# Output projections of the attention stages summed block by block between the attention's own work, in four banks, and idle products kept in the second half of the rows only

## The chip, the cores and the metric

One core of one Trainium2 chip runs the whole program. The time is device microseconds (us) for one execution. The time before is the median of three runs.

## What is computed

Two transformer blocks, one after the other, on 512 rows of 1024 features in float32. The first block (an attention, a recurrence, a convolution and a mixture that gathers 128 rows of two tables for each token) is not changed. The second block has two layers; each is a mixer, a cross attention on 256 memory rows, and a gated feed-forward part, and each of the three adds into the residual X:

```python
for layer in range(DEPTH_2):
    x = x + mixers[layer](rms_norm(x, mix_norms[layer]))     # ends in o @ w_out
    x = x + memory_cross_attention(rms_norm(x, xn), ...)      # ends in o @ w_o
    x = x + swiglu(rms_norm(x, fn), wg, wu, wd)
```

The even mixer (layer 0) has 8 heads of sliding-window attention and 8 heads of latent attention; the odd one (layer 1) has 16 heads of dilated attention; the cross attention has 4 heads of 128. The products that end the first two lines, `o @ w_out` and `o @ w_o`, are the "projections onto X" of this case.

## The kernel before

Each engine has its own program, written by the same generators, and they meet through semaphores (`p.wait_ge`, and `p.claim`, which waits for the last user of a bank or a weight slot). Every engine takes its instructions in the order written.

**Two halves.** The second block runs twice, on rows 0 to 255 (the first half, `h == 0`) and on rows 256 to 511 (the second half, `h == 1`). The first half is woven into the end of the first block's table gathers (`peer_steps`, `Beside`): POOL issues the gathers, DVE multiplies and adds the gathered rows (lines L2361 and L2375), and between them all engines take steps of `second_pe`, `second_act`, `second_dve` for half 0 in a fixed proportion of costs. In this execution that is about 1943 to 3145 us. The second half runs alone, from there to the end.

**Attention units.** An attention stage is a list of units (one head, 128 query rows): 32 in each mixer, 8 in each cross attention. For unit u the order on PE is: scores of u+1 (L2955), a piece of "fill", transposes of the weights of u (L2964), output of u-1 (L2973), and, where a block of 128 output columns is complete, its transpose into `a.o` (L2979, the store). DVE and ACT take the minimum, the exponent and the copies. The fill is PE work from a generator (`latent_pe`, `dilated_pe`: projections that later units need) of which `Fill.take` hands out `rate` steps a unit; a step `"after", n` is held until unit n. The steps are numbered the same way on ACT and DVE, which only yield there.

**Idle products.** Where a unit got little fill, `occupied` (L2658) issues a product of the identity by itself into bank 0, whose result nobody reads. It does so too, 8 at a time, before and after the row norm's products (`scale_pe`, L2733), and 2 before a rotation.

**Projection onto X.** `out_pe` runs after the last unit. It goes over four column groups i of 256, each with its own weight load of 1024 KB (512 KB in the cross attention), into banks 6 and 7 by turns; each group takes two chains over all blocks c of `a.o` (8, or 4 in the cross attention), by L2687. DVE adds group i into X (L2721) while PE is at group i+1, ACT squares it (L2706), DVE sums the squares (L2713), and `scale_pe` needs all of that.

**Weights** land in four wide slots taken in turn (`next_wide`); SP issues a load when the last user of the slot has ended (`load_wide`), in program order.

## Time and profile before

| | |
|---|---|
| median of 3 runs | 4248.45 us (4247.49 to 4258.28) |
| the profiled execution: its time, its span | 4260.14 us, 4258.3 us |
| PE busy | 3555.5 us (83%) |
| DVE, POOL, ACT busy | 2219.7, 1379.1, 711.5 us |
| mean granted clock of TensorE | 0.910 |
| second block, first half, beside the gathers | about 1943 to 3145 us |
| second block, second half, alone | about 3160 to 4258 us |

A granted clock of 1.0 in a row is TensorE at 2.4 GHz, 0.5 is 1.2 GHz, and a value between is a mean over a stretch that had both. A logical float32 product shows as two MATMUL records, so x8 in the order of a program is x16 in a timeline.

### The profile page before, as it was taken

The numbers are of one execution on the slowest core, as the hardware profiler recorded it, in microseconds if no ns is written. First come the engines' busy times: TensorE is split into PE (matmuls) and PEld (weight loads), VectorE is DVE, ScalarE is ACT, GpSimd is POOL, SyncE is SP. The second block draws the span as 40 slices with busy tenths as digits, with TensorE's granted clock in tenths as the row PEclk, the third lists the DMA queues.
The fourth block names the chain that finished last, engine by engine and source line by source line (L and its number), as shares of the span: only waits on it lengthen the run. The fifth ranks groups of instructions, "written<-read, shape, count | busy, mean of one in ns | idle before, by whom it ended". The sixth has DMA issues, their size and how long they took to land. (4 is left out here: it accounts for less than half of the span.)

```text
span 4258.3 us, 41827 instructions
## 1 busy us (share of the span) xinstructions
PE 3555.5 (83%) x15638; PEld 2641.1 (62%) x15638; DVE 2219.7 (52%) x4375; ACT 711.5 (17%) x1582; POOL 1379.1 (32%) x1215
## 2 busy tenths in 40 slices
PE   7888997888667677866788898888978899999999
PEld 3446557786323343425567776677766678877787
DVE  2443134445887878777667668777642420033201
ACT  2212122221211111111221001210011210012100
POOL 0550012221566666765235655445500000000000
PEclk9888988999888898979788999799988999999999
DMA  6320300004899899998567999779941134421343
GB/s 197 96 81 11 95 21 1 1 12 135 290 331 331 327 355 334 361 334 296 172 223 280 394 386 352 249 262 383 394 156 57 40 96 152 148 79 60 99 150 108
DMA packets 452351, 835.74 MB, mean 196 GB/s; under 512 B 46707, under 2 KB 294574, under 8 KB 452142
## 3 DMA queue, kind: packets, MB, share of 16 engines
q0 software_dynamic: 147456, 536.94, 34.3%
q1 hardware_dynamic: 304694, 296.13, 21.9%
q8 instruction: 125, 2.05, 0.2%
q14 instruction: 76, 0.62, 0.0%
HBM read 830.80 MB, written 2.17 MB: 196 GB/s over the span
## 5 line engine op out<-in xcount | busy, mean ns | idle before, releaser
L2687 PE MATMUL banks<-arena 128*128 128x256 f32 (+1 forms) x4992 | 1142.1, 388 | 78.3 <-DMA arena<-in_l_w_up 35.4
L2687 PEld LDWEIGHTS banks<-arena 128*128 128x128 f32 (+1 forms) x4992 | 954.9, 194 | 254.3 <-issue 40.9
L2246 POOL DMA_INDIRECT arena<-in_peer_u,arena x512 | 569.2, 1112 | 578.2 <-DVE arena L2375 226.3
L2246 POOL DMA_INDIRECT arena<-in_peer_v,arena x512 | 588.8, 1150 | 446.0 <-DVE arena L2361 284.9
L2375 DVE CUSTOM_DVE_ANT_0 arena<-arena 128x1024 f32<-128x1024 f32 x512 | 627.9, 1226 | 106.1 <-DMA arena<-in_peer_u,arena 89.1
L2319 PE MATMUL banks<-arena 128*128 128x512 f32 x768 | 419.6, 690 | 233.1 <-ACT arena L2337 150.0
L2319 PEld LDWEIGHTS banks<-arena 128*128 128x128 f32 x768 | 156.6, 217 | 461.0 <-issue 265.7
L2361 DVE SCALAR_TENSOR_TENSOR arena<-arena 128x1024 f32<-128x1024 f32 x316 | 406.2, 1286 | 34.9 <-DMA arena<-in_peer_v,arena 24.9
L3465 PE MATMUL banks<-arena 128*128 128x256 f32 x1408 | 310.4, 378 | 0.0
L3507 DVE TENSOR_TENSOR arena<-banks,arena 128x512 f32<-128x512 f32 x44 | 30.4, 692 | 526.7 <-PE banks L2687 526.3
L3465 PEld LDWEIGHTS banks<-arena 128*128 128x128 f32 x1408 | 265.6, 189 | 38.3
L2658 PE MATMUL banks<-arena 128*128 128x128 f32 x1088 | 189.0, 302 | 0.0
L2658 PEld LDWEIGHTS banks<-arena 128*128 128x128 f32 x1088 | 171.3, 217 | 22.2 <-issue 16.9
L835 PE MATMUL banks<-arena 128*128 128x512 f32 (+1 forms) x320 | 134.1, 567 | 28.4 <-ACT arena L962 11.7
L3486 ACT ACTIVATE arena<-banks 128x512 f32<-128x512 f32 x44 | 26.3, 599 | 698.5 <-PE banks L2687 698.4
L548 PE MATMUL banks<-arena 128*128 128x512 f32 (+1 forms) x384 | 142.1, 530 | 0.0
L3002 ACT ACTIVATE arena<-arena 128x256 f32<-128x256 f32 (+3 forms) x128 | 69.4, 542 | 374.1 <-DVE arena L3041 271.2
L2955 PE MATMUL banks<-arena 64*128 64x256 f32 (+6 forms) x384 | 124.8, 430 | 3.0 <-issue 2.3
L2063 PE MATMUL banks<-arena 128*128 128x512 f32 (+1 forms) x320 | 119.8, 526 | 3.5 <-ACT arena L1841 3.5
L835 PEld LDWEIGHTS banks<-arena 128*128 128x128 f32 x320 | 63.3, 207 | 92.9 <-issue 81.4
L1566 POOL TENSOR_TENSOR arena<-arena 64x256 f32<-64x256 f32 x24 | 19.1, 796 | 313.4 <-ACT arena L1465 312.5
L510 POOL TENSOR_TENSOR arena<-arena 128x2048 f32<-128x2048 f32 x16 | 57.3, 3603 | 194.0 <-ACTq L278 105.5
(330 smaller groups left out, 4326.4 us busy)
## 6 DMA issues: line engine op xcount, KB each, us to landing
arena<-in_l_w_gate SPq DMA_DIRECT2D x44, 1024.0 KB, 6.7
arena<-in_l_w_up SPq DMA_DIRECT2D x44, 1024.0 KB, 10.0
arena<-in_l_w_down SPq DMA_DIRECT2D x44, 1024.0 KB, 5.5
arena<-in_ada_w SPq DMA_DIRECT2D x24, 1024.0 KB, 8.1
arena<-in_l_w_qkv SPq DMA_DIRECT2D x24, 1024.0 KB, 8.2
arena<-in_w_in SPq DMA_DIRECT2D x36, 512.0 KB, 4.0
arena<-in_l_w_out SPq DMA_DIRECT2D x16, 1024.0 KB, 5.3
arena<-in_peer_q_w SPq DMA_DIRECT2D x20, 512.0 KB, 7.1
```

The source lines that it names most:

```text
L548: ins = p.e.matmul(k.bank[b][0:m, 0:n], k.W[slot][:, c, 0:m], rhs(c), start=c == 0, stop=c == c_n - 1, skip_group_check=True)
L835: ins = p.e.matmul(k.bank[b][0:m, 0:n], k.W[slot][:, c, 0:m], rhs(c), start=c == 0, stop=c == c_n - 1, skip_group_check=True)
L2063: ins = p.e.matmul(k.bank[4][:, cols], ws[j][:, c, :], k.HT[:, c, cols], start=c == 0, stop=c == DC - 1, skip_group_check=True)
L2246: p.e.indirect_dma_start(e.ring[slot], None, tables[table], bass.IndirectOffsetOnAxis(ap=e.IDX[h][:, t, j:j + 1], axis=0)).then_inc(*p.up( ...
L2319: ins = p.e.matmul(k.bank[b], e.diag[x % 4], e.ring[slot][:, half * T:half * T + T], start=h == 0 and j == 0, stop=h == HEADS - 1 and j == ...
L2361: p.e.scalar_tensor_tensor(out=e.ACC[t], in0=e.ring[slot], scalar=factor, in1=e.ACC[t], op0=ALU.mult, op1=ALU.add).then_inc(*p.up(S.rows_a ...
L2375: p.e.tensor_tensor_reduce(out=e.prod, in0=e.ring[slot], in1=e.H2[:, t, :], scale=1.0, scalar=0.0, op0=ALU.mult, op1=ALU.add, accum_out=e. ...
L2658: p.e.matmul(k.bank[0][:, 0:P], k.ident, k.ident, start=True, stop=True, skip_group_check=True)
L2687: ins = p.e.matmul(out, left(c), right(c), start=c == 0, stop=c == c_n - 1, skip_group_check=True)
L2955: ins = p.e.matmul(k.bank[b][:, c0:c0 + keys.shape[1]], x.q, keys, start=True, stop=True, skip_group_check=True)
L3002: p.e.activation(s[:, 0:x.nb], s[:, 0:x.nb], ACT.Exp, bias=low, scale=-1.0, accum_out=cols[:, 2:3]).then_inc(*(p.up(S.weights_exp, key) if ...
L3465: ins = p.e.matmul(k.bank[4 + o // 2][:, o % 2 * TH:o % 2 * TH + TH], w[:, r, P * o:P * o + P], a.hid[:, (i - 1) % 2, TH * r:TH * r + TH], ...
```

## The change

`out_pe` is cut in two. The blocks of `a.o` but the last are multiplied as soon as they are stored, as more fill among the units (`out_begun_pe`, `out_more_pe`); `out_pe` keeps the last block only. Since every block now adds into all four column groups, four banks (0, 1, 6, 7) stay open and all four weight slots are held from the first block to the last product.

```diff
+OUT_BANKS = 0, 1, 6, 7
+FIRST_PAIRS, LAST_PAIRS = (0, 1), (2, 3)
+WINDOWS_OUT, LATENTS_OUT = range(4), range(4, 7)
+def even_rate(u):
+    return 1 if u < 24 else 3
+def out_begun_pe(k, p, a, tag, stores, w, parts, cs):
+    for i in parts:
+        w[i] = landed_wide(k, p, (tag, i)).rearrange("p (c n) -> p c n", n=256)
+    for c in cs:
+        yield "after", stores[c][1] + 3
+        for stored in stores[c][0]:
+            p.wait_ge(*stored)
+        for i in parts:
+            bank = k.bank[OUT_BANKS[i]]
+            if c == 0:
+                p.claim(("bank", OUT_BANKS[i]), k.S.residual_added, (tag, i))
+            for x in range(2):
+                p.e.matmul(bank[:, TH * x:TH * x + TH], w[i][:, c, P * x:P * x + P], a.o[:, c, :], start=c == 0 and x == 0,
+                           stop=False, skip_group_check=True)
+            if i % 2:
+                yield 4 * MM
...
-def occupied(k, p, n):
+def occupied(k, p, a, n, b):
+    if a.h_id == 0:
+        return
+    if ("bank", b) in p.over:
+        p.wait_ge(*p.over["bank", b])
     for _ in range(n):
-        p.e.matmul(k.bank[0][:, 0:P], k.ident, k.ident, start=True, stop=True, skip_group_check=True)
+        p.e.matmul(k.bank[b][:, 0:P], k.ident, k.ident, start=True, stop=True, skip_group_check=True)
...
-    yield from units_pe(k, p, a, ("even", h), even_units(k, a), Fill(latent_pe(k, p, a)), 1)
-    yield from out_pe(k, p, a, ("mix", h), stores_of(k, ("even", h), even_units(k, a)))
+    begun = lambda parts, cs: out_begun_pe(k, p, a, ("mix", h), stores, w, parts, cs)
+    fill = chain(latent_pe(k, p, a, begun(FIRST_PAIRS, WINDOWS_OUT)), begun(LAST_PAIRS, WINDOWS_OUT),
+                 out_more_pe(k, p, a, stores, w, LATENTS_OUT))
+    yield from units_pe(k, p, a, ("even", h), units, Fill(fill), even_rate)
+    yield from out_pe(k, p, a, ("mix", h), stores, w, (DC - 1,))
...
-            yield from units_pe(k, p, a, ("dil", h), dilated_units(k, a), Fill(dilated_pe(k, p, a)), 2)
+            fill = chain(dilated_pe(k, p, a), out_begun_pe(k, p, a, ("l1_out", h), stores, w, range(4), range(DC - 1)))
+            yield from units_pe(k, p, a, ("dil", h), units, Fill(fill), dilated_rate)
...
-        yield from cross_pe(k, p, a, l)
-        yield from units_pe(k, p, a, ("cross", l, h), cross_units(k, a, l), none(), 0)
+        yield from cross_pe(k, p, a, l, 0)
+        fill = chain(cross_pe(k, p, a, l, 1), [("cross", l, h)], out_begun_pe(k, p, a, ("xo", l, h), stores, w, range(4), range(3)))
+        yield from units_pe(k, p, a, ("cross", l, h), units, Fill(fill), cross_rate)
```

ACT and DVE get the same steps without the products. In the cross attention the second half of the query projection (`cross_pe(..., 1)`) moves among the units too. The idle products are 544 in the second block before (282 in the first half, 262 in the second), and none and 208 after. The sum of the step costs that sets the proportion of gathers to second-block work is the same.

Lines of the changed kernel that stand in the rows below: L2808 and L2831 are the products moved among the units, L2845 those left in `out_pe`, L2692 is L2687, L2663 is L2658, L2738 is L2733, and L3021, L3030, L3039, L3045 are scores, weights, output and store.

**Place 1.** PE, dilated attention of the second half, where the query, key and value projections have run out. Before, a unit there has idle products only:

```order
L2955 MATMUL banks<-arena 128x256 [waits scores_low]
L2955 MATMUL banks<-arena 128x256
L2979 MATMUL banks<-arena 128x128 [waits act_weights,output_scaled]
L2658 MATMUL banks<-arena 128x128
L2964 MATMUL banks<-arena 128x128 [waits dve_stored,weights_exp]
L2964 MATMUL banks<-arena 128x128 x2
L2658 MATMUL banks<-arena 128x128
L2973 MATMUL banks<-arena 128x64 x3
```

After, the last step of the value projection is followed, one unit further on, by block 0 of the projection (the four rows of a unit between are left out):

```order
L3021 MATMUL banks<-arena 128x256 [waits scores_low]
L3021 MATMUL banks<-arena 128x128
L2692 MATMUL banks<-arena 128x256 x8
L3021 MATMUL banks<-arena 128x256 [waits scores_low]
L3021 MATMUL banks<-arena 128x256
L3045 MATMUL banks<-arena 128x128 [waits act_weights,output_scaled]
L2808 MATMUL banks<-arena 128x256 [waits landed_wide3,landed_wide0,landed_wide2,landed_wide1]
L2808 MATMUL banks<-arena 128x256 x3
L2808 MATMUL banks<-arena 128x256 [waits values_ready]
L2808 MATMUL banks<-arena 128x256
L2808 MATMUL banks<-arena 128x256 [waits rotated]
L2808 MATMUL banks<-arena 128x256
```

What was two idle products is now 8 products in four banks, and ahead of them PE waits for four weight slots.

**Place 2.** PE, cross attention of the second half, layer 1. Before, the whole query projection stands ahead of the units:

```order
L2687 MATMUL banks<-arena 128x256 [waits residual_added,landed_wide2]
L2687 MATMUL banks<-arena 128x256 x15
L2955 MATMUL banks<-arena 128x256 [waits cross_ready]
L2955 MATMUL banks<-arena 128x256 [waits norm_root]
L2658 MATMUL banks<-arena 128x128
L2964 MATMUL banks<-arena 128x128 [waits weights_exp]
L2964 MATMUL banks<-arena 128x128
```

After, its last four products stand among the units, and the next scores wait for `cross_ready` and for all four weight slots:

```order
L2692 MATMUL banks<-arena 128x256 x4
L3030 MATMUL banks<-arena 128x128 [waits act_stored,weights_exp]
L3030 MATMUL banks<-arena 128x128
L3039 MATMUL banks<-arena 128x128 x2
L2692 MATMUL banks<-arena 128x256 x4
L3021 MATMUL banks<-arena 128x256 [waits landed_wide2,landed_wide1,cross_ready,landed_wide0,landed_wide3]
L3045 MATMUL banks<-arena 128x128 [waits act_weights,output_scaled]
L2808 MATMUL banks<-arena 128x256 [waits dve_stored]
L2808 MATMUL banks<-arena 128x256 x3
```

The wait for the weights of the projection has moved from behind the units to unit 4.

**Place 3.** PE, end of the dilated stage of the second half. Before, the last store is followed by 64 products:

```order
L2979 MATMUL banks<-arena 128x128 [waits output_scaled]
L2687 MATMUL banks<-arena 128x256 [waits landed_wide1]
L2687 MATMUL banks<-arena 128x256 x6
L2687 MATMUL banks<-arena 128x256 [waits dve_stored]
L2687 MATMUL banks<-arena 128x256 x8
L2687 MATMUL banks<-arena 128x256 [waits landed_wide2]
L2687 MATMUL banks<-arena 128x256 x15
L2687 MATMUL banks<-arena 128x256 [waits residual_added,landed_wide3]
L2687 MATMUL banks<-arena 128x256 x15
L2687 MATMUL banks<-arena 128x256 [waits residual_added,landed_wide0]
L2687 MATMUL banks<-arena 128x256 x15
L2658 MATMUL banks<-arena 128x128 x8
```

After, it is followed by 8, which wait for the copy of that store:

```order
L3045 MATMUL banks<-arena 128x128 [waits output_scaled]
L2845 MATMUL banks<-arena 128x256 [waits dve_stored]
L2845 MATMUL banks<-arena 128x256 x7
L2663 MATMUL banks<-arena 128x128 [waits scores_low]
L2663 MATMUL banks<-arena 128x128 x7
L2738 MATMUL banks<-arena 128x256 [waits scores_low,residual_squared,residual_summed]
L2738 MATMUL banks<-arena 128x256 x3
```

The norm's four products (L2738) now stand 16 instructions behind the last store.

## Rows read from the trace of the kernel before

**Rows 1.** Windows by stage: busy us (instructions) by engine, granted clock, DMA share, GB/s
```profile
2031.00:2196.00 165.00, 118.01 (x483) 87.25 (x482) 102.03 (x267) 39.47 (x125) 37.34 (x39) 0.74 0.51 158
...
2250.00:2286.00 36.00, 24.48 (x106) 19.58 (x105) 20.38 (x45) 8.61 (x26) 8.90 (x10) 0.62 0.55 189
...
2723.00:2771.00 48.00, 39.22 (x147) 30.85 (x148) 28.99 (x81) 11.25 (x35) 14.93 (x13) 0.57 0.58 186
...
3245.00:3396.00 151.00, 120.65 (x578) 82.20 (x578) 61.62 (x209) 46.25 (x128) 0.00 (x0) 0.90 0.09 28
...
3881.00:3918.00 37.00, 30.78 (x211) 26.28 (x212) 15.77 (x54) 11.01 (x29) 0.00 (x0) 1.00 0.04 15
```

**Rows 2.** Timeline of PE, dilated attention of the second half: start, us, line, what, idle
```profile
3868.70 3.62 PE L2687 MATMUL banks<-arena 128*128 128x256 f32 x16
...
3874.38 3.72 PE L2687 MATMUL banks<-arena 128*128 128x256 f32 x16
...
3880.42 0.39 PE L2658 MATMUL banks<-arena 128*128 128x128 f32 x2
...
3881.55 0.52 PE L2964 MATMUL banks<-arena 128*128 128x128 f32 x3 [0.74 <-DVE arena L3074]
...
3917.74 27.89 PE L2687 MATMUL banks<-arena 128*128 128x256 f32 x128
...
3947.24 1.92 PE L2733 MATMUL banks<-arena 128*128 128x256 f32 x8
```

**Rows 3.** Timeline of PE, end of a feed-forward part of the second half
```profile
3717.15 1.95 PE L2658 MATMUL banks<-arena 128*128 128x128 f32 x16
...
3721.43 1.97 PE L2733 MATMUL banks<-arena 128*128 128x256 f32 x8 [2.33 <-ACT arena L2706]
```

**Rows 4.** Timeline of PE, even mixer of the second half
```profile
3324.95 0.39 PE L2658 MATMUL banks<-arena 128*128 128x128 f32 x2
...
3338.55 2.76 PE L3271 MATMUL banks<-arena 128*96 128x256 f32 x12
...
3374.83 0.39 PE L2658 MATMUL banks<-arena 128*128 128x128 f32 x2
...
3395.35 1.90 PE L2687 MATMUL banks<-arena 128*128 128x256 f32 x8
```

**Rows 5.** Timeline of PE, cross attention of the second half, layer 1
```profile
3966.61 1.03 PE L2955 MATMUL banks<-arena 128*128 128x256 f32 x4
...
3978.78 0.41 PE L2964 MATMUL banks<-arena 128*128 128x128 f32 x2 [0.87 <-ACT arena L3017]
...
3980.54 0.39 PE L2658 MATMUL banks<-arena 128*128 128x128 f32 x2
...
3989.87 14.02 PE L2687 MATMUL banks<-arena 128*128 128x256 f32 x64
...
4005.51 1.96 PE L2733 MATMUL banks<-arena 128*128 128x256 f32 x8
```

**Rows 6.** DMA issues of the second half alone: KB each, median us to landing
```profile
arena<-in_l_w_out SPq DMA_DIRECT2D x8, 1024.0 KB, 5.1
...
arena<-in_l_w_xo SPq DMA_DIRECT2D x8, 512.0 KB, 3.3
```

**Rows 7.** The same for the first half, beside the gathers
```profile
arena<-in_l_w_gate SPq DMA_DIRECT2D x22, 1024.0 KB, 19.4
...
arena<-in_l_w_out SPq DMA_DIRECT2D x8, 1024.0 KB, 9.4
```

**Rows 8.** Timeline of PE, first half: a wait and the speed after it
```profile
2955.46 8.77 PE L2687 MATMUL banks<-arena 128*128 128x256 f32 x32 [4.90 <-DMA arena<-in_l_w_up]
...
2964.07 6.21 PE L3465 MATMUL banks<-arena 128*128 128x256 f32 x28
...
1968.51 3.75 PE L2733 MATMUL banks<-arena 128*128 128x256 f32 x8 [9.84 <-DVE arena L2713]
```

**Rows 9.** Idle products of the first half: window of line L2658 alone
```profile
2031.00:2196.00 165.00, 33.24 (x138) 27.83 (x138) 0.74 0.51 158
```

More of the change, by code:

```diff
@@ new lines, in out_begun, with out_more_pe @@
+def out_begun(stores, parts, cs):
+    for c in cs:
+        yield "after", stores[c][1] + 3
+        for i in parts:
+            if i % 2:
+                yield 4 * MM
+def out_more_pe(k, p, a, stores, w, cs):
+    for c in cs:
+        yield "after", stores[c][1] + 3
+        for stored in stores[c][0]:
+            p.wait_ge(*stored)
+        for i in range(4):
+            for x in range(2):
+                p.e.matmul(k.bank[OUT_BANKS[i]][:, TH * x:TH * x + TH], w[i][:, c, P * x:P * x + P], a.o[:, c, :], start=False,
+                           stop=False, skip_group_check=True)
+            if i % 2:
+                yield 4 * MM
@@ L2788, in out_act, with out_pe @@
+def out_pe(k, p, a, tag, stores, w, cs):
+    for c in cs:
+        for stored in stores[c][0]:
+            p.wait_ge(*stored)
     for i in range(4):
         for x in range(2):
-            yield from product_pause(chunks)
+            for c in cs:
+                ins = p.e.matmul(k.bank[OUT_BANKS[i]][:, TH * x:TH * x + TH], w[i][:, c, P * x:P * x + P], a.o[:, c, :], start=False,
+                                 stop=c == cs[-1], skip_group_check=True)
+            if x:
+                ins.then_inc(*p.up(k.S.proj_filled, (tag, i)))
+            yield MM * len(cs)
@@ L2791, in out_act @@
+def out_act(k, p, a, tag, cs):
+    for i in range(4):
+        for x in range(2):
+            yield MM * len(cs)
             if i and x == 0:
@@ L2922, in stores_of @@
         if x.ends:
-            out.setdefault(x.block, []).append(((k.S.act_stored, k.S.dve_stored)[x.tile % 2], (name, u)))
+            out.setdefault(x.block, ([], u))[0].append(((k.S.act_stored, k.S.dve_stored)[x.tile % 2], (name, u)))
+            out[x.block] = out[x.block][0], u
     return out
@@ L2936, in units_pe @@
             filled = 0
-            for n in fill.take(rate, min(u + 1, len(units) - 1)):
+            for n in fill.take(rate(u), min(u + 1, len(units) - 1)):
                 filled += n
@@ L2988, in units_act @@
         if step == "fill":
-            yield from fill.take(rate, min(u + 1, len(units) - 1))
+            yield from fill.take(rate(u), min(u + 1, len(units) - 1))
         elif step == "rest":
@@ L3026, in units_dve @@
         if step == "fill":
-            yield from fill.take(rate, min(u + 1, len(units) - 1))
+            yield from fill.take(rate(u), min(u + 1, len(units) - 1))
         elif step == "rest":
@@ L3086, in rotate_pe @@
     n = out.shape[1]
-    occupied(k, p, 2)
+    occupied(k, p, a, 2, 1 if key[0] == "in" else 4)
     p.wait_ge(k.S.raw_ready, key)
@@ L3234, in latent_sp, with latent_pe @@
               ("latent_k", h, 3, 1))
-def latent_pe(k, p, a):
+def latent_pe(k, p, a, between):
     S, h = k.S, a.h_id
@@ L3288, in latent_pe, with latent_act @@
         yield "latent", h, i
-def latent_act(k, p, a):
+        if i == 1:
+            yield from between
+def latent_act(k, p, a, between):
     S, h = k.S, a.h_id
@@ L3324, in latent_act, with latent_dve @@
         yield "latent", h, i
+        if i == 1:
+            yield from between
 def latent_last(a, i):
     return ("even", a.h_id), 16 + 4 * i + 3
-def latent_dve(k, p, a):
+def latent_dve(k, p, a, between):
     S, h = k.S, a.h_id
@@ L3362, in latent_dve @@
         yield "latent", h, i
+        if i == 1:
+            yield from between
 def even_units(k, a):
@@ L3425, in cross_units @@
                  None, None, [(k.S.cross_ready, ("cross", l, a.h_id, i // 2))], (k.S.mem_ready, (l, 7)), True,
[L3426 removed]
+                 a.o[:, i, P * t:P * t + P], i, ("cross", l, a.h_id) if i >= 2 else None) for i in range(4) for t in range(2)]
 def ffn_sp(k, p, a, l):
@@ L3667, in second_pe @@
     p.turn = 0
-    none = lambda: Fill(iter(()))
     yield from experts_pe(k, p, a, ("experts", h))
@@ L3703, in second_act @@
     yield from inputs_act(k, p, a)
-    yield from units_act(k, p, a, ("even", h), even_units(k, a), Fill(latent_act(k, p, a)), 1)
-    yield from out_act(k, p, a, ("mix", h))
+    units = even_units(k, a)
+    stores = stores_of(k, ("even", h), units)
+    fill = chain(latent_act(k, p, a, out_begun(stores, FIRST_PAIRS, WINDOWS_OUT)), out_begun(stores, LAST_PAIRS, WINDOWS_OUT),
+                 out_begun(stores, range(4), LATENTS_OUT))
+    yield from units_act(k, p, a, ("even", h), units, Fill(fill), even_rate)
+    yield from out_act(k, p, a, ("mix", h), (DC - 1,))
     for l in range(2):
@@ L3731, in second_dve @@
     yield from inputs_dve(k, p, a)
-    yield from units_dve(k, p, a, ("even", h), even_units(k, a), Fill(latent_dve(k, p, a)), 1)
-    yield from out_dve(k, p, a, ("mix", h))
+    units = even_units(k, a)
+    stores = stores_of(k, ("even", h), units)
+    fill = chain(latent_dve(k, p, a, out_begun(stores, FIRST_PAIRS, WINDOWS_OUT)), out_begun(stores, LAST_PAIRS, WINDOWS_OUT),
+                 out_begun(stores, range(4), LATENTS_OUT))
+    yield from units_dve(k, p, a, ("even", h), units, Fill(fill), even_rate)
+    yield from out_dve(k, p, a, ("mix", h), (DC - 1,))
     for l in range(2):
```

111 lines of the change are left out of this document (58 added, 53 removed).

## The prediction

> **What bounds the kernel now.** The table of the profile comes first: PE is busy 83% of the span, the others 52% and less. Then the windows by stage, because an average says little here. In the second half of the second block (from about 3160 us) nothing but PE, its clock and the waits inside the attention matter: in the dilated units without fill PE is busy 30.8 of 37 us, some of it with idle products, DVE 15.8 and ACT 11.0, and the DMA share is 0.04 [rows 1]. In the first half the same units stand between gathered rows on DVE and take longer: 48 us instead of 37, at a granted clock of 0.57 instead of 1.00, and the even mixer 165 us instead of 151, at 0.74 instead of 0.90 [rows 1]. PE's clock is down there while PE is working, and the gathers leave DMA time over (share 0.51 to 0.58). The timeline of PE then shows what the change can win: the piece of a unit that no work covers. It is small, since a unit has only about 1.2 us of it.
>
> **Prices used everywhere.** 64 products of the projection take 27.89 us, so one is 0.434 us and one block c (8 products) 3.5 us [rows 2]. The stage from the last store to the norm's products is 3947.24 - 3917.74 = 29.5 us in a mixer [rows 2] and 4005.51 - 3989.87 = 15.6 us in a cross attention [rows 5].
>
> After the change that stage has 8 products. Its adds can't hide behind products any more: DVE adds, ACT squares, DVE sums, by turns. The end of a feed-forward part has this chain already, with four banks ending 0.87 us apart: 3721.43 - 3717.15 = 4.3 us from the last product to the norm's [rows 3]. Before, it was 1.8 us of idle products. The first of the 8 also waits for the last store's copy, which 8 products of older blocks covered before; a wait for that copy was 0.74 us [rows 2]. So the stage is 3.5 + 4.3 + 0.7 = 8.5 us. **A mixer** moves 56 products, 24.3 us: 24.3 + 8.5 - 29.5 = +3.3 us before anything is covered. **A cross attention** moves 24, 10.4 us: 10.4 + 8.5 - 15.6 = +3.3 us. That is a debt of 3.3 us in each of eight places, and units have to pay it back.
>
> Products that go over four banks by turns cost nothing extra: the down projection does that and runs 28 records in 6.21 us, 0.22 us each like the others [rows 8].
>
> **Second half, part by part.**
>
> Dilated: a unit with 8 products took 3874.38 - 3868.70 = 5.7 us, so its own work is 2.2; eleven without took 3917.74 - 3880.42 = 37.3, or 3.4 each [rows 2]. The 1.2 us between them are waits and idle products. Seven units get a block: -8.3. The fourth weight slot is that of the last value projection, so its load starts when that has ended and lands 5.1 us later [rows 6], one unit (2.2) of which is covered: +2.9, with all units queued behind that wait. 3.3 - 8.3 + 2.9 = **-2.1**.
>
> Even: the fill has room at two places. Four windowed units get 4 products (1.7 us) each; five took 3338.55 - 3324.95 = 13.6, 2.7 each [rows 4]; with own work of about 1.5 (rows of the cross attention, below) they become 3.2, so 6.9 us of products cost 2.0: -4.9. Of the last six units (3395.35 - 3374.83 = 20.5, 3.4 each, own work 2.2 as in the dilated ones) three get products: -3.6. The last weight slot is that of the key up-projection, which ends directly ahead of the wait: +5.1 [rows 6], and a wait of that length was followed by 8.77 us where 32 records take 7.0: +1.8 [rows 8]. 3.3 - 4.9 - 3.6 + 5.1 + 1.8 = **+1.7**.
>
> Cross: 8 units took 3989.87 - 3966.61 = 23.3 [rows 5]; a unit's own work is 3980.54 - 3978.78 = 1.8 less one idle product of 0.2, say 1.5 [rows 5]. Of 11 us free, the last unit's 1.2 stay: -9.8, filled with the 7 us of query products and 10.4 of the projection. Against it +3.3, +0.8 for the first scores, which now follow the ACT copy of their own queries at once (as a store's copy, 0.74), and +3.3 for the load of 512 KB into the slot of the second query part [rows 6]. **-2.4, twice: -4.8.**
>
> Sum of the second half: -2.1 + 1.7 - 4.8 = -5.2 us.
>
> **First half.** The same, and four differences.
>
> Longer units. They are 11 us longer in the dilated stage [rows 1], 7 of 11 are filled: -7. In the even mixer 14 us, 7 of 32: -3. In the first cross attention 36 us instead of 23 [rows 1]; DVE has gathered rows among these units, so of 13 us I take half, twice: -13.
>
> Slower loads. A projection's load lands after 9.4 us beside the gathers, not 5.1 [rows 7]: +4.3 in each mixer; in the cross attentions, where the DMA share is 0.55, I take 3 of the 6 us more: +6. Together +15. Also the four slots now come free within 3.5 us and not over 30, and the first feed-forward load (19.4 us to landing [rows 7]) is wanted 3.5 + 4.3 + about 6 us of norm later: some 5 us late; that stage fetches at the limit anyway, so +3 in all.
>
> No idle products. In the even mixer they are 69 (138 records), 33 us busy [rows 9]; records overlap, so some 16 us of PE, half of it in waits that stay: -8, and with the rest of the first half -10.
>
> The clock. Around a norm PE now rests for the whole chain. After a rest of 9.84 us the norm's 8 records took 3.75 us where they take 1.92 [rows 2, 8]: +1.8, and about +1 for the first products behind it (of the 1.8 of rows 8, part was there before). Six norms: +17, of which 5 are inside feed-forward stages that wait for weights: +12.
>
> Sum: -5.2 - 23 + 15 + 3 - 10 + 12 = -8 us.
>
> TensorE: Matmul & The Clock Gate (Part 1, The HAM clock gate) in the Trainium skill says that the low clock is the default and that activity releases it. By that rule taking idle products out of a stage whose clock is already 0.74 speaks against this change; my sum has it at the norms only, and with it in the units too the sum would be the second rival's. The trace agrees as far as rows 8 go.
>
> **Total:** -5.2 - 8 = -13 us on a profiled execution of 4260.1 us (span 4258.3), that is 4247. The median of the runs is 4248.45, 11.7 below that execution, so I put the difference on the median: **4236 us**. One execution more or less differs by about 0.3%, 12.7 us, and less than that is no change.
>
> **Rivals.**
>
> Clock low in the first half (slower). The units' own small products alone don't bring the clock back. PE was busy 118 us in the even mixer's window, 85 without the idle products' 33, at 0.74 [rows 1, 9]; at 0.5 it is 85 x 0.74 / 0.5 = 126, +41 us, less what lies in waits. 4236 + 41 = 4277 at most; at a mean of 0.62 it is +16, 4252. It decides from +25 us on, a clock under 0.57 there. For it: 0.57 in the dilated window although idle products ran. Against: units with real fill have more work, not less. Chance 0.21.
>
> Clock high in the first half. The moved products bring the clock to 1.0 where it is 0.57 to 0.74: the even window's 85 us become 63 (-22), the dilated window's own share of 39 becomes some 12 less; with the credits above, 4236 - 34 = 4202. For it: where fill of L2687 runs, the second half has 1.00. Chance 0.23.
>
> Loads eat the gain. The four waits last their full landing in both halves (5.1 and 9.4 us, none covered), and the feed-forward loads come 5 us late for each of gate and up: +3 in the second half, +12 in the first, 4251: no change. Chance 0.14.
>
> **How the numbers follow.** The forecast (4229 to 4244) has 0.42, half of it beyond 0.3%. Faster: 0.22 + 0.23 = 0.45. Same: 0.20, 0.12 of the loads' case and 0.02 of the low clock's, 0.34. Slower: 0.19 + 0.02 = 0.21. The low end of unknown costs is every credit in full and a clock of 1.0 (4198), the high end the low clock for most of the even mixer (4264); outside lie 2 in 10.
>
> **What would show it.** Right: from last store to the norm's products 8.5 us in the second half; a wait of PE for w_out of about 5 us late in the even mixer and 3 in the dilated stage, for w_xo 3 in each cross attention; units with 8 products at 5.7 us; norm products at 3.7 us in the first half. Wrong: a granted clock of the window of the first even mixer under 0.6 or over 0.9, or a chain of adds that is much longer where gathered rows stand between them on DVE.

## The result: 1.1% slower

The changed kernel took 4304.60 us (median of 4 runs, 4298.10 to 4309.00), the kernel before 4247.97 us (4 runs): a ratio of 1.0112, 95% interval 1.0084 to 1.0139. The prediction was 4236 us and a range to 4264, so it was wrong in sign and out of its range. The profiled execution took 4309.00 us, 48.9 more than that of before.

The head of the profile's page after the change (busy time, share, instructions, and the granted clock of PE in 40 slices):

```profile
span 4307.1 us, 40453 instructions
...
PE 3518.1 (82%) x14966; PEld 2580.3 (60%) x14966; DVE 2220.7 (52%) x4375; ACT 713.4 (17%) x1582; POOL 1363.6 (32%) x1215
...
PEclk9887988998888898888688998889988999999999
```

PE is busy 37 us less than before (no idle products in the first half), and the span is 49 us longer. So PE rests some 86 us more. The list of PE's waits (total, times, longest) names where:

```profile
PE banks L2738 <- ACT arena L2711: 48.6, 10, 13.4
...
PE banks L2738 <- issue: 21.0, 5, 7.3
PE banks L3021 <- DMA arena<-in_l_w_xo: 20.1, 4, 8.2
...
PE banks L2808 <- DMA arena<-in_l_w_out: 16.7, 3, 7.0
```

20.1 and 16.7 us are waits for the weights of the projections, which PE never waited for before. A fourth rest, 5.24 us before 3405.53, is put down to "issue" in the timeline. It is a wait for w_out too: the fourth load of w_out was issued at 3400.32 and landed at 3405.44. That makes 42.0 us in all. L2738 is the norm's products: their rests were 35.0 us before and are 69.6 here, which is most of the remainder.

Now the same stretches as in [rows 1] (the window ends are shifted, since everything comes later), and two pieces of the dilated tail by themselves:

```profile
core 0: us, PE busy (x) PEld busy (x) DVE busy (x) ACT busy (x) POOL busy (x), PEclk, DMA share, GB/s
2031.00:2219.00 188.00, 130.98 (x452) 90.01 (x450) 119.80 (x288) 39.73 (x125) 54.19 (x54) 0.70 0.57 180
2263.00:2300.00 37.00, 25.85 (x99) 19.61 (x100) 20.78 (x40) 3.65 (x13) 11.24 (x11) 0.77 0.55 171
2747.00:2810.00 63.00, 45.29 (x190) 35.68 (x190) 40.83 (x90) 8.15 (x29) 30.70 (x24) 0.80 0.65 213
3268.00:3447.00 179.00, 146.07 (x659) 103.38 (x658) 61.33 (x208) 46.70 (x128) 0.00 (x0) 0.89 0.07 24
3917.00:3983.00 66.00, 59.53 (x295) 49.90 (x295) 15.75 (x53) 11.47 (x29) 0.00 (x0) 0.87 0.02 7
3926.00:3954.00 28.00, 28.00 (x153) 23.84 (x151) 6.66 (x23) 5.44 (x14) 0.00 (x0) 1.00 0.00 1
3954.00:3968.00 14.00, 11.83 (x48) 9.62 (x47) 3.90 (x13) 2.63 (x8) 0.00 (x0) 0.62 0.00 0
```

The clock of the first even mixer is 0.70 and not far from the 0.74 of [rows 1]; in the cross attention and the dilated mixer of the first half it is higher than before (0.77 and 0.80, where it was 0.62 and 0.57). What the reader should see is the second half. There the dilated tail ran at 1.00 before; now it has 0.87, and behind 28 us in which PE is full come 14 us at 0.62.

The timeline of PE shows how a rest and a low clock go together. A row is start, duration, operation, and in brackets the rest before it:

```profile
3398.36 1.93 PE L3350 MATMUL banks<-arena 128*64 128x512 f32 x4 [0.95 <-DVE arena L3169]
3405.53 3.75 PE L2808 MATMUL banks<-arena 128*128 128x256 f32 x8 [5.24 <-issue]
...
3455.40 3.53 PE L2738 MATMUL banks<-arena 128*128 128x256 f32 x8 [2.29 <-issue]
...
3757.21 1.97 PE L2738 MATMUL banks<-arena 128*128 128x256 f32 x8 [2.33 <-ACT arena L2711]
...
3919.12 5.38 PE L2808 MATMUL banks<-arena 128*128 128x256 f32 x16 [2.74 <-DMA arena<-in_l_w_out]
...
3926.44 3.72 PE L2808 MATMUL banks<-arena 128*128 128x256 f32 x16
...
3932.15 3.62 PE L2808 MATMUL banks<-arena 128*128 128x256 f32 x16
...
3956.74 0.49 PE L2663 MATMUL banks<-arena 128*128 128x128 f32 x2 [1.44 <-ACT arena L3083]
...
3958.02 1.81 PE L3039 MATMUL banks<-arena 128*128 128x64 f32 x8
...
3967.93 5.24 PE L2808 MATMUL banks<-arena 128*128 128x256 f32 x16 [0.73 <-DVE arena L3140]
...
3982.39 0.33 PE L3045 MATMUL banks<-arena 128*128 128x128 f32 x1 [0.45 <-DVE arena L3134]
3983.10 3.72 PE L2845 MATMUL banks<-arena 128*128 128x256 f32 x16 [0.39 <-DVE arena L3140]
...
3990.90 3.16 PE L2738 MATMUL banks<-arena 128*128 128x256 f32 x8 [2.29 <-issue]
...
4020.22 1.19 PE L3021 MATMUL banks<-arena 128*128 128x256 f32 x2 [3.68 <-DMA arena<-in_l_w_xo]
...
4022.19 3.69 PE L2808 MATMUL banks<-arena 128*128 128x256 f32 x8 [0.57 <-DVE arena L3140]
...
4027.44 1.89 PE L2808 MATMUL banks<-arena 128*128 128x256 f32 x8
...
4031.22 1.99 PE L2808 MATMUL banks<-arena 128*128 128x256 f32 x8 [0.38 <-DVE arena L3140]
...
4034.77 1.89 PE L2808 MATMUL banks<-arena 128*128 128x256 f32 x8
```

8 records of L2808 take 1.89 us at full clock. Behind the waits of 5.24 and 3.68 us they take 3.7; behind the one of 2.74 us, 16 records take 5.38 us where they take 3.72 otherwise. The norm's products take 3.2 to 3.5 us behind an attention, where the same instructions took 1.92 before [rows 2].

**Where the time went, by stage.** A stage is taken from the start of one norm's 8 records to the next in the timeline (1970.28, 2229.81, 2309.26 and so on; before: 1968.51, 2227.86, 2301.44). Ahead of 1970.28 the change lost 1.8 us. From there to the first norm of the mixer in the second half (3211.53, before 3188.58) it lost 21.2, and from there to the last norm (4293.08, before 4243.80) 26.3, or 26.4 as the sum of the rounded stages:

| stage | first half | second half | predicted, second half |
|---|---|---|---|
| even mixer | +0.2 | +7.6 | +1.7 |
| cross attention, layer 0 | +5.9 | +3.7 | -2.4 |
| feed-forward, layer 0 | +1.8 | +1.5 | 0 |
| dilated mixer | +8.4 | +7.9 | -2.1 |
| cross attention, layer 1 | +4.6 | +4.1 | -2.4 |
| feed-forward, layer 1 | +0.2 | +1.6 | 0 |

(The two joints between the halves are +0.2 and 0.0.) Each kind of attention loses, in both halves. The second half, beside which no rows are gathered, is the cleaner one to explain.

### The profile page after: what moved, and what is told of

It is laid out like the page before. It is cut to its first block and busy times, and to the rows that moved or that the text cites. A ratio compares the mean times of both kernels' runs of the same rounds, so it can differ in the third digit from the quotient of the medians.

```text
span 4307.1 us, 40453 instructions
## 1 busy us (share of the span) xinstructions
PE 3518.1 (82%) x14966; PEld 2580.3 (60%) x14966; DVE 2220.7 (52%) x4375; ACT 713.4 (17%) x1582; POOL 1363.6 (32%) x1215
## 3 DMA queue, kind: packets, MB, share of 16 engines
q8 instruction: 120, 1.97, 0.2%
## 5 line engine op out<-in xcount | busy, mean ns | idle before, releaser
L2692 PE MATMUL banks<-arena 128*128 128x256 f32 x4224 | 982.7, 391 | 81.9 <-DMA arena<-in_l_w_up 36.5
L2692 PEld LDWEIGHTS banks<-arena 128*128 128x128 f32 x4224 | 817.1, 196 | 237.2 <-issue 53.9
L2246 POOL DMA_INDIRECT arena<-in_peer_v,arena x512 | 574.9, 1123 | 469.7 <-DVE arena L2361 311.4
L2319 PEld LDWEIGHTS banks<-arena 128*128 128x128 f32 x768 | 159.6, 221 | 460.1 <-issue 265.2
L3535 PE MATMUL banks<-arena 128*128 128x256 f32 x1408 | 310.4, 378 | 0.0
L3535 PEld LDWEIGHTS banks<-arena 128*128 128x128 f32 x1408 | 265.6, 189 | 38.3
L2808 PE MATMUL banks<-arena 128*128 128x256 f32 x544 | 153.5, 439 | 31.9 <-DMA arena<-in_l_w_out 16.7
L2808 PEld LDWEIGHTS banks<-arena 128*128 128x128 f32 x544 | 117.3, 223 | 58.7 <-issue 25.4
L3021 PE MATMUL banks<-arena 64*128 64x256 f32 (+6 forms) x384 | 124.4, 429 | 22.9 <-DMA arena<-in_l_w_xo 20.1
L3556 ACT ACTIVATE arena<-banks 128x512 f32<-128x512 f32 x44 | 26.3, 598 | 696.1 <-PE banks L2692 696.0
L3134 DVE TENSOR_SCALAR arena<-banks,arena 128x64 f32<-128x64 f32 (+1 forms) x160 | 47.6, 298 | 157.0 <-PE banks L3039 152.2
L3123 DVE COPY arena<-banks 128x128 f32<-128x128 f32 (+2 forms) x80 | 36.6, 457 | 173.8 <-PE banks L3030 173.8
```

The source lines that it names most:

```text
L2246: p.e.indirect_dma_start(e.ring[slot], None, tables[table], bass.IndirectOffsetOnAxis(ap=e.IDX[h][:, t, j:j + 1], axis=0)).then_inc(*p.up( ...
L2319: ins = p.e.matmul(k.bank[b], e.diag[x % 4], e.ring[slot][:, half * T:half * T + T], start=h == 0 and j == 0, stop=h == HEADS - 1 and j == ...
L2692: ins = p.e.matmul(out, left(c), right(c), start=c == 0, stop=c == c_n - 1, skip_group_check=True)
L2808: p.e.matmul(bank[:, TH * x:TH * x + TH], w[i][:, c, P * x:P * x + P], a.o[:, c, :], start=c == 0 and x == 0, stop=False, skip_group_check ...
L3021: ins = p.e.matmul(k.bank[b][:, c0:c0 + keys.shape[1]], x.q, keys, start=True, stop=True, skip_group_check=True)
L3535: ins = p.e.matmul(k.bank[4 + o // 2][:, o % 2 * TH:o % 2 * TH + TH], w[:, r, P * o:P * o + P], a.hid[:, (i - 1) % 2, TH * r:TH * r + TH], ...
```

## The experiments

Twelve kernels. Ratios are to the kernel before, timed on the same chip; the chips differ (the kernel before had medians of 4248, 4267, 4280 and 4257 us), so the ratios count, not the microseconds. Stage numbers are read as in the table above, and are of one profiled execution each. In the second half they repeat to 0.8 us where the code is the same, with three exceptions: the feed-forward part of layer 0 came out at 0.0 once and at +1.5 or +1.6 three times, and in the kernel before without idle products in its first half the cross attention of layer 0 took 2.6 us and the dilated mixer 23.7 us longer (told at the end). In the first half they repeat badly: the first half of the change gave +21 and +8 us in two profiles, and that of the kernel before came out 6.9 us shorter in a second one.

### Are idle products and the clock of the first half the cause?

Two kernels. The change with its idle products in both halves:

```diff
-    if a.h_id == 0:
-        return
```

> The changed kernel, with its idle products issued in both halves of the rows (the change issued none in the first half). Theory A, the waits for the weight loads of the projections make the loss (PE waits 26.8 us for them in the first half and 15.2 us in the second): the idle products move the time by less than 4 us, about 4304. Theory B, the missing idle products let the granted clock fall in the first half (0.70 in the even mixer where it was 0.74, norm products 3.3 to 3.6 us where they took 1.92): at least 10 us come back, 4294 or less, and the norm products there take 1.9 us again.

Ratio 1.0093 (1.0061 to 1.0126), which can't be told from 1.0112. The first half lost 21.7 us against 21.2. By the ratios anything from nothing to some 25 us may have come back, by the stages nothing did. Theory B falls with its other part too: the six norms behind a stage of the first half took 2.6 to 3.8 us, not 1.9, with idle products around them. These idle products come with the change's banks and waits, which the next but one experiment takes by themselves.

And the kernel before, without the idle products of its first half:

```diff
+    if a.h_id == 0:
+        return
```

> The kernel before, with only the idle products of the first half left out. Theory A (waits for loads): no difference over 0.3% from the kernel before, 4248. Theory B (clock): the clock falls without them, 10 us or more slower, 4258 or more. The prediction's own terms were -10 for the products and +12 for the norms, +2 together.

Ratio 0.9971 (0.9946 to 0.9996), if anything faster. The mean granted clock over all runs fell from 0.906 to 0.899, and the first half got 12.4 us shorter. The lower clock cost nothing that could be seen. The expectation had -10 and +12 here, +2 in all. The +12 had no occasion in this kernel: behind the attentions the whole projection still stands ahead of the norm, and the norm's products took 1.97 us as before. So -12.4 is to be set against the -10 alone, and agrees with it within the scatter of the first half. My slower rival (low clock in the first half) finds no support.

### The idle products' banks

The kernel before, with the change's banks and waits for the idle products:

```diff
+    if ("bank", b) in p.over:
+        p.wait_ge(*p.over["bank", b])
-        p.e.matmul(k.bank[0][:, 0:P], ...
+        p.e.matmul(k.bank[b][:, 0:P], ...
```

> The kernel before, with only the banks of the idle products as in the change (2, 4 and 5, 1 at the inputs) and the wait for the last user of that bank ahead of each. If an idle product can stand behind that wait as well as ahead of it: 4248, within 0.3%. Rival: the idle product that stood in the gap of a unit now stands behind it, the granted clock falls in the units that have no other fill as it did for 14 us in the changed kernel's second dilated stage (0.62), 8 us or more slower, 4256 or more.

Ratio 1.0049 (1.0020 to 1.0077), 21 us: the rival, not the main expectation. In the second half the even mixer lost 4.6 us, the dilated one 4.0, each cross attention 1.4. Two things make this up. In a unit the idle product stood in the rest, ahead of the wait; now it waits for a reader of its bank and stands behind it. In the dilated mixer, where [rows 2] has 0.39 us of idle products at 3880.42 and then 0.74 us of rest, the same place is now

```profile
3902.82 0.49 PE L2661 MATMUL banks<-arena 128*128 128x128 f32 x2 [0.88 <-DVE arena L3077]
3903.15 0.49 PE L2967 MATMUL banks<-arena 128*128 128x128 f32 x3
```

L2661 is the idle product. That costs 0.1 to 0.2 us a unit, 1.3 us over the eleven units there and 1.4 in a cross attention. The other part is the clock. At a rotation in the even mixer the kernel before has its idle products ahead of the rest, and this run has them behind it:

```profile
3361.16 0.61 PE L2658 MATMUL banks<-arena 128*128 128x128 f32 x4
3363.38 1.10 PE L3089 MATMUL banks<-arena 96*96 96x512 f32 x2 [1.62 <-ACT arena L3081]
...
3365.20 1.00 PE L2973 MATMUL banks<-arena 128*128 128x64 f32 x8
```

```profile
3374.67 0.71 PE L2661 MATMUL banks<-arena 128*128 128x128 f32 x4 [1.59 <-ACT arena L3020]
3375.21 1.14 PE L3092 MATMUL banks<-arena 96*96 96x512 f32 x2
...
3377.86 1.75 PE L2976 MATMUL banks<-arena 128*128 128x64 f32 x8
```

L3020 is ACT's copy out of bank 4. The rests are of one length, but the eight records behind them take 1.75 us and not 1.00; the window over these units has a clock of 0.84 (3371 to 3403), where it was 1.00 before (3358 to 3388). It isn't so at every such place: at a rotation of the dilated mixer (a rest of 1.53 us, 1.48 before) the 8 records of a projection behind it took 2.75 us, and 2.76 before. Of the dilated mixer's 4.0 us, 2.5 came ahead of the first idle product that waits for its bank: the norm's products and the first projections ran at the low clock there (2.81 us for the norm, 1.97 before), behind a rest of 2.33 us that both kernels have. That part is chance and not the banks, as the last section shows. So some 9 us of the 11.4 are a piece of the change that I had not priced.

With four banks held open there is no bank without another engine in it; the Trainium skill's PSUM — Partial Sum Buffer (Terms) says that two engines may not be in one bank of one quadrant at once, which no run here shows.

The other way round, the changed kernel with its idle products in bank 0 again, without a wait (while the sum stands open there, they multiply by a block of zeros):

```diff
+    left, begins = k.ident, True
+    if b in (4, 5):
+        b = 0
+        if getattr(p, "begun", False):
+            left, begins = k.K["causal"][:, 0:P], False
```

> The changed kernel, where the idle products of the units and rotations go to bank 0 without a wait again; while the projection's sum stands open there they multiply by zeros and add nothing. Theory D, an idle product behind the claim of bank 4 or 5 is on the path (the kernel before lost 4.6 us in the second even mixer, 4.0 in the dilated one and 1.4 in each cross attention by it): with some 100 such products left in the second half 4 to 6 us come back there, about 0.1% of the time, mostly in the two mixers. Rival: it was the clock by chance, nothing comes back in those stages.

The ratio, 1.0084 (1.0055 to 1.0114), can't tell it from the change, but the stages can: even mixer +3.1 us and not +7.6, the dilated one +7.3 and not +7.9, the cross attentions +3.8 and +3.7. The whole second half is +20.6 and not +26.4. The 5.8 us that came back were expected (4 to 6), but not "mostly in the two mixers": 4.5 are in the even one, where the change too has an idle product behind a rest of 1.59 us ahead of a rotation and a low clock after it. Where products fill the units there is little.

### The waits for weights

The changed kernel, with the identity in place of the weights in the products that were moved:

```diff
-                p.e.matmul(bank[:, TH * x:TH * x + TH], w[i][:, c, P * x:P * x + P], a.o[:, c, :], ...
+                p.e.matmul(bank[:, TH * x:TH * x + TH], k.ident, a.o[:, c, :], ...
```

> The changed kernel, where the products moved among the units take the identity matrix in place of the loaded weights, so that they wait for no load (only the last block's products still do, when the loads have long landed). The output is not the projection's; number, shape and place of all products are those of the change. Theory A (waits for loads): 42 us of waits go, and some 5 to 8 us of half clock behind them, 4254 to 4265, close to the kernel before. Rival C, the units have no room for the products and the waits only stand where PE would have waited for DVE anyway: less than 20 us come back, over 4285.

Ratio 0.9973 (0.9942 to 1.0003): against 1.0112, 1.4% or 59 us, where 47 to 50 were expected. The two intervals together leave some 17 us either way, but the stages say the same: PE's 42.0 us of waits were worth more than themselves, in the second half 23.8 us for 15.2. In the second half the even mixer went from +7.6 to -0.3 for a wait of 5.24 us, the cross attentions from +3.7 and +4.1 to -2.3 and -2.2 for 3.53 and 3.68 us. The dilated one stayed at +5.7, and the feed-forward part of layer 0 at +1.6.

Where does the wait have to stand? In `out_begun_pe` the four waits come when the generator is asked for its next step. In a cross attention that is ahead of the scores of unit 4, long before the first product is due. One edit moves them:

```diff
-    for i in parts:
-        w[i] = landed_wide(...)
     for c in cs:
         yield "after", stores[c][1] + 3
...
         for i in parts:
+            if i not in w:
+                w[i] = landed_wide(...)
```

> The changed kernel, where only one thing is moved: each column group's wait for its weight load stands ahead of its own first product, and no longer all of them ahead of the first unit's hold. Order and number of products are the change's. If the place of the wait is what costs in the cross attentions: their PE waits of 3.5 us in the second half and 8.2 and 4.8 in the first go nearly all, with half clock behind them 2 to 3 us each, some 25 us in all, 4280; the mixers, whose last group is wanted at once, keep most of theirs. If only the other order helps: under 8 us.

Ratio 1.0013 (0.9983 to 1.0043). I expected 25 us and got about 42 (the two intervals together leave some 17 either way): the place of one kind of wait is worth about as much as the whole loss. That doesn't make it the only cause: the second half is still +11.2 us, and the first half, which has no idle products now, came out at -9.3. In the second half the cross attentions are at -1.8 and -1.4, the feed-forward parts behind them at 0.0; PE waits for no w_xo at all. In the dilated mixer the wait went too, against the expectation. The even mixer keeps its wait and is +8.9:

```profile
3374.43 2.08 PE L2808 MATMUL banks<-arena 128*128 128x256 f32 x4 [4.07 <-DMA arena<-in_l_w_out]
...
3380.57 6.81 PE L2808 MATMUL banks<-arena 128*128 128x256 f32 x24
...
3453.69 1.99 PE L2808 MATMUL banks<-arena 128*128 128x256 f32 x8 [0.67 <-DVE arena L3140]
```

The wait is shorter (4.07 us), but the low clock behind it lasts longer: 24 records take 6.81 us, 5.35 in the change. The row at 3453.69 is the first block of the cross attention, at full clock.

### The dilated mixer's 14 us at 0.62

Not the wait: without it the stage was +5.7 (identity) and +5.5 (waits at use), and the low clock in the same units was still there, 0.67 and 0.69 over 14 us. The change with another order in this mixer alone:

```diff
 def dilated_rate(u):
-    return 2
+    return 1 if u in (20, 21, 23, 24, 26, 27) else 2
...
-    chain(dilated_pe(k, p, a), out_begun_pe(..., range(4), range(DC - 1)))
+    chain(dilated_pe(k, p, a), out_begun_pe(..., FIRST_PAIRS, (0, 1)), out_begun_pe(..., LAST_PAIRS, (0, 1)),
+          out_begun_pe(..., range(4), range(2, DC - 1)))
```

> The changed kernel with the new order in the dilated mixer alone (blocks 0 and 1 of groups 0 and 1 first, waits at use, four products to a unit more evenly). Theory A with the clock: in the second half's dilated mixer the wait of 2.7 us and the low clock behind the filled units (0.62 for 14 us) both go, 12 to 15 us of the stage; in the first half's 8 to 14; ratio 1.005 or less. Rival: the low clock in that stage comes by chance, and only the waits go, 3 and 7 us, ratio 1.009.

Ratio 1.0049 (1.0025 to 1.0074), and the stage went from +7.9 to -5.3 us in the second half, from +8.4 to -8.5 in the first. The window over the same units, and the last products:

```profile
3875.00:3945.00 70.00, 67.59 (x380) 56.96 (x379) 22.08 (x71) 15.64 (x39) 0.00 (x0) 1.00 0.09 31
```

```profile
3932.88 3.72 PE L2809 MATMUL banks<-arena 128*128 128x256 f32 x16
...
3951.53 1.97 PE L2738 MATMUL banks<-arena 128*128 128x256 f32 x8 [2.29 <-issue]
```

The clock is 1.00, and the last moved block takes 3.72 us where it took 5.24. The products are the same, but every unit now has four or eight of them. In the change six units were full and then two had only idle products, and the clock fell in those two (in the change behind a rest of 1.44 us, 3956.74; the window reads 0.62 to 0.69 in all six profiles with this order). What about the order does it isn't shown: eleven units in a row with idle products only ran at 1.00 in the kernel before [rows 2].

### Is the loss of each half its own?

The change in the second half alone; the first half is the kernel before:

```diff
+    if h:
         yield from units_pe(..., Fill(fill), even_rate)
         yield from out_pe(k, p, a, ("mix", h), stores, w, (DC - 1,))
+    else:
+        yield from units_pe(..., Fill(latent_pe(k, p, a, ())), lambda u: 1)
+        yield from whole_pe(...)
```

> The change in the second half of the rows alone; the first half is the kernel before, with its idle products and whole projections. By the trace of the changed kernel the second half lost 26 us: ratio 1.006 to the kernel before, the other half of the loss being the first half's. Rival: the second half is longer only because of what the first half leaves (loads and slots in another order), then the ratio is 1.000.

Ratio 1.0071 (1.0052 to 1.0090), and the stages of the second half are those of the change to 0.1 us: +7.6, +3.8, +1.6, +7.8, +4.1, +1.6. The rival falls, and the rest of the loss is the first half's.

### A version that beats both

The waits at their use, the new order in the dilated mixer, and in the even mixer blocks 4 and 5 of groups 0 and 1 ahead of groups 2 and 3, so that the last load lands behind work:

```diff
 def even_rate(u):
-    return 1 if u < 24 else 3
+    return 1 if u < 24 else 3 if u == 24 else 1 if u == 25 else 2
...
+    chain(latent_pe(..., begun(FIRST_PAIRS, WINDOWS_OUT)), begun(FIRST_PAIRS, (4, 5)), begun(LAST_PAIRS, range(6)),
+          out_more_pe(k, p, a, stores, w, (6,)))
```

> The changed kernel, with the same products in another order: each column group waits for its weight load only ahead of its own first product; in the even mixer blocks 4 and 5 of groups 0 and 1 come ahead of everything of groups 2 and 3; in the dilated one blocks 0 and 1 of groups 0 and 1 first; and from there on units get four products each more evenly, not eight or none. Theory A (waits): of the 42 us that PE waited for the loads some 30 or more go, with the half clock behind them: 4250 to 4272. Rival C (no room in the units): under 15 us come back, 4290 or more.

Ratio 0.9925 (0.9908 to 0.9943). That is 1.9% or 79 us under the change, where the expectation had 32 to 55. The even mixer of the second half is at -1.7, the dilated one at -7.0, the cross attentions at -1.1 and -2.3.

To this the idle products in bank 0 without a wait, as above:

```diff
+        b = 0
+        if getattr(p, "begun", False):
+            left, begins = k.K["causal"][:, 0:P], False
```

> Both edits, the new order and the idle products in bank 0 without a wait. Theory A and D together: 4245 to 4268, 4 to 6 us under the new order alone, and in the second half the two mixers no longer than in the kernel before.

Ratio 0.9953 (0.9926 to 0.9980), and -8.1 us for the second half where it was -10.6: the 4 to 6 us that were expected under the new order alone did not come. Once the units are filled evenly, the bank gives nothing that can be told. Then more idle products ahead of a norm:

```diff
-    occupied(k, p, a, 8, 2)
+    occupied(k, p, a, 16, 2)
     p.wait_ge(S.residual_summed, (source, 2))
```

> As the run before it, with 16 idle products ahead of each norm's products in the second half in place of 8, to cover the chain of adds and squares (PE stood 2.3 us there, and the norm's 8 records took 3.5 us where they take 1.97). If the clock falls for that rest: 1.5 us for each of the four norms behind a projection, 6 us less. If the extra products only push the norm's own back: 0 to 6 us more.

Ratio 0.9896 (0.9877 to 0.9914). The rest ahead of the norm's products is 0.50 us and they take 1.97, behind the even mixer for one:

```profile
3433.39 1.97 PE L2743 MATMUL banks<-arena 128*128 128x256 f32 x8 [0.50 <-issue]
```

The six norms of the second half all take 1.97 us, and the second half is -12.9 us, 4.8 better, about as expected. By the ratios it is 24 us better than the kernel before it; the stages don't show where the rest of that is. At last the same in the first half:

```diff
-    if a.h_id == 0:
+    if a.h_id == 0 and b != 2:
         return
```

> The fastest kernel so far (new order, idle products in bank 0, 16 ahead of the norms), with the idle products around the norms and the expert sums of the first half as well. If the clock at the norms matters there too: the norm products take 1.97 us where they took 3.2 to 3.75, some 1.5 us for each of six norms, up to 9 us faster. If the first half is set by the gathers and their arithmetic: no difference beyond 0.3%.

Ratio 0.9926 (0.9893 to 0.9960), mean clock 0.91. The norms behind the first half's stages run at 1.97 us now, too, and no gain of it can be told from none. That agrees with a first half that goes by its gathers; no run tests this by itself. These four kernels are 0.5 to 1.0% faster than the kernel before, and 1.6 to 2.1% faster than the change.

## Why the prediction was wrong, step by step

**What held.** The stage from the last store in the dilated mixer: 8.5 us predicted, 3982.39 to 3990.90 is 8.5. The length of the waits: 5.1, 2.9 and twice 3.3 predicted in the second half, 5.24, 2.74, 3.53 and 3.68 measured. In the first half 9.4, 7.2 and twice 6.3 (29 in all), measured 7.04, 6.88, 8.17 and 4.75 (26.8). A unit with 8 products: 5.7 us, measured 5.71 (3926.44 to 3932.15). The idle products left out of the first half: -10, and -12.4 in the run that did only that. The norm's products in the first half: 3.7 us predicted, 2.8 to 3.6 measured.

**What failed: a wait was priced at its length and a rest at nothing.** The second half came out at +26.4, not -5.2, and the runs split these 31.6 us (each share is a difference of single profiles, good to about 1 us, and they need not add up as neatly as they do):

- The dilated mixer, 10.0 us. I took the cost of a filled unit (5.7) and an unfilled one (3.4) from a stretch with idle products in each unit at clock 1.00 [rows 2], and took them to hold in any order. With six full units followed by two empty ones the clock fell. The new order gave -5.3 us, which is what my credits (3.3 - 8.3 = -5.0) say; the wait itself cost 2.4, and 2.9 was priced.
- The credit of the cross units, 8.2 us. "-9.8" for 11 us free was too much. With the waits at their use the two stages are -1.8 and -1.4, where my terms without the wait give -5.7. Units with four products take 3.8 and 3.6 us in the change (4027.44, 4031.22, 4034.77), not 3.2: without the products' 1.73 us a unit takes 1.8 to 2.1, with rests of 0.3 to 0.4 us for DVE, and I had taken 1.5. Another 0.6 and 1.0 us of it are the norm's products at the low clock ahead of the query products (2.48 and 2.90 us in the run with the waits at their use, 1.92 before).
- The wait in the cross attentions, 7.5 us. Twice 3.3 was priced, and moving it gave 5.5 us in each stage, half as much again as its length, since the products behind it run at half clock. The other 3.1 us are 1.5 and 1.6 in the feed-forward parts behind: their norm's products took 3.5 us and not 1.97. With the wait eight such norms of ten were slow, without it three of eight, so that these 3.1 us are the wait's is likely and not shown.
- The even mixer, 5.9 us. 4.5 are the idle products behind a claim of a bank, a part of the diff that I described and gave no price. The wait cost 7.9, and 6.9 was priced, since there I had added 1.8 for the clock. The last 0.4 is open.

These are 31.6 us. I had the rule in the rows: behind a rest of 4.90 us 32 records took 8.77 and not 7 [rows 8]. I used it for one wait in the second half, and for norms in the first half only. The norms behind the attentions of the second half were slow too (3.2 to 3.5 us behind rests of 2.29 to 2.34).

**The first half** came out at +21 in this profile (+8 in another of the same code), not -8. Taking the waits away made it -18, so they cost some 39 us there (26 by the other profile), where 29 were priced. What my terms leave without waits is -8 - 29 = -37; -18 came. This gap of 19 us need not lie in a term of the first half: its sum starts from the second half's, whose credits for the dilated and the cross units were 10.5 and 8.2 us too large by the runs above. Whether the -23 for longer units was right isn't shown, and one profile for each kernel doesn't settle it, given that scatter.

**The rivals.** "Loads eat the gain" (0.14, 4251 us) named the right mechanism, and priced it at the loads' own time. "Clock low in the first half" (the first in the list, though the prediction once calls it the second) had the right sign, and the runs speak against it: the clock of the first even mixer was 0.70, not under 0.6, and idle products in both halves brought nothing back. No rival held what happened: the loads' waits, the low clock behind them and the low clock in the gaps between full units, in both halves.

## What to carry to other kernels

Work that is moved among other work brings its waits with it: put each wait directly ahead of the first instruction that needs it, and look at what an in-order engine then holds up. Price a wait of TensorE at its length plus what the next products lose at half clock, here about half as much again (5.5 us for 3.6, 7.9 for 5.2). Spread moved work evenly: four or eight products in each unit kept the clock, eight in six units and none in the next two lost it.

## What the runs showed of the hardware

The longer TensorE rested, the surer was the low clock behind it, and in the middle it was chance. The norm's 8 records in the second half, over all profiles: behind a rest of 0 to 1.13 us they took 1.97 us or less in 25 cases of 25; behind a rest of 2.08 to 2.34 us in 28 cases of 59, and 2.5 to 3.65 us in the others; the first norm of this half, behind 3.8 to 6.0 us, was longer in all 14 profiles (2.4 to 3.75 us). Behind a wait of 3.5 us or more for a load (15 in five profiles with all waits ahead of the first product) the next 8 records of the moved products always came at half clock (3.1 us from the first start to the last, and 1.5 at full clock). What stood ahead doesn't decide the middle: the same norm behind the same feed-forward part took 1.97 us in the change (3757.21) and

```profile
3731.05 3.62 PE L2738 MATMUL banks<-arena 128*128 128x256 f32 x8 [2.34 <-ACT arena L2711]
```

in the run with the new order in the dilated mixer, whose instructions in the second half up to there are those of the change. The Trainium skill, TensorE: Matmul & The Clock Gate (Part 1, The HAM clock gate), says that the clock follows how busy PE has been recently; the short and the long rests agree, and the rows do not show what decides between them.

And the clock can fall by chance. In the run of the kernel before without idle products in the first half, the second dilated mixer, whose code was not touched, took 23.7 us longer:

```profile
3840.00:3880.00 40.00, 38.35 (x200) 31.72 (x198) 12.57 (x34) 7.71 (x22) 0.00 (x0) 0.96 0.18 61
3880.00:3920.00 40.00, 36.60 (x160) 30.97 (x159) 11.62 (x39) 9.37 (x24) 0.00 (x0) 0.63 0.08 27
3920.00:3940.00 20.00, 18.67 (x68) 15.44 (x69) 5.16 (x17) 2.48 (x6) 0.00 (x0) 0.50 0.00 1
```

PE is busy 92% of the last 60 us, and the clock is 0.63 and 0.50; that execution took 4282.26 us where the median of its ten was 4247.43. In the kernel before, the same units ran at 1.00 [rows 1]. Why it stays low while PE is busy isn't settled here. It is one reason why a stage's time from one profile needs the medians beside it. Another is the first block, which no kernel here touches: the first norm of the second block came at 1953.1 us before, and at 1970.9 to 1986.5 in the four kernels that were timed on one of the other chips.
